# Narrow projections as column strips, and matrix memory's first products ahead of an output gate slot

## The reference, cut to what matters

```python
p = _split(h @ w_in[l])       # a_cq 256, a_ckv 128, a_krope 32, ..., c_qidx 256, c_kidx 32, c_widx 8, ...
k_rope = _rope(p["a_krope"])  # one 32-wide key for all 4 heads
score  = relu(einsum('bqhd,bkd->bqhk', qidx, kidx))         # 8 index heads, one 32-wide index key
index  = einsum('bqh,bqhk->bqk', widx, score) * idx_scale   # 8 index weights per token
```

```python
aq, ak, av, mq, mk, mv, mo, mg = split(h @ w_in)   # mg: 16 gate columns; mo: 512 output gate columns
i_f, f_f, i_b, f_b = mg + gate_b                   # per token
h_m = mlstm(mq, mk, mv, i, log_sigmoid(f))         # forward and backward, summed
h_m = rms_norm(h_m) * sigmoid(mo)
```

## Time and profile before

| | |
|---|---|
| median of 3 runs | 1643.64 us (1638.76 to 1643.98) |
| the profiled execution | 1640.14 us |
| its span | 1638.5 us |
| mean granted TensorE clock | 0.957 |
| TensorE busy | 1507.0 us, 92% |
| VectorE, ScalarE, GpSimd busy | 569.5, 340.9, 93.9 us |
| HBM | 223 GB/s over the span |

### The profile page before, as it was taken

One profiled execution on the slowest core, in us unless ns is written; L12 is line 12 of the kernel. 1 busy time (PEld: TensorE's weight loads), 2 busy tenths in 40 slices (PEclk: granted clock), 3 DMA queues, 4 the chain that ended last, 5 costly groups with the idle time before them and its releaser, 6 DMA issues.

```text
span 1638.5 us, 27188 instructions
## 1 busy us (share of the span) xinstructions
PE 1507.0 (92%) x11479; PEld 1080.2 (66%) x11479; DVE 569.5 (35%) x1400; ACT 340.9 (21%) x788; POOL 93.9 (6%) x144
## 2 busy tenths in 40 slices
PE   6999999999879999999987799999869998999997
PEld 5777777877644576756436799998746675555554
DVE  2514332523443415706414111111056733233233
ACT  1222211222232113217113000000042214010000
POOL 0010000010100000012002000000010000000000
PEclk8899999999989989998998999999979999999999
DMA  8365535475574621065522999999785043999997
GB/s 268 88 209 177 181 98 145 127 233 181 178 215 143 205 77 52 27 215 165 189 82 104 342 388 389 400 396 395 296 291 196 27 154 117 385 385 386 380 388 284
DMA packets 188237, 367.00 MB, mean 224 GB/s; under 512 B 19101, under 2 KB 145913, under 8 KB 172273
## 3 DMA queue, kind: packets, MB, share of 16 engines
q1 hardware_dynamic: 171552, 322.90, 55.5%
q0 software_dynamic: 10544, 32.48, 6.3%
q10 hardware_dynamic: 6048, 10.31, 1.8%
HBM read 345.26 MB, written 20.41 MB: 223 GB/s over the span
## 4 chain that ended last, share of the span: by engine, by line
PE 78%; DMA 8%; DVE 7%; ACT 4%; issue 1%; SPq 1%; POOL 0%; POOLq 0%; DVEq 0%; ACTq 0%
PE ps_proj L652 30%; PE ps_outp L652 9%; PE ps_proj L1270 7%; PE ps_outp L1270 7%; PE ps_score L1270 6%; DMA ring<-in_exp_w 6%; PE ps_outp L1215 3%; PE ps_outp L1371 2%; PE ps_proj L778 2%; PE ps_score L823 1%; PE ps_turn L805 1%; SPq L3142 1%; PE ps_proj L1117 1%; DMA ring<-in_w_in 1%; PE ps_score L1077 1%
## 5 line engine op out<-in xcount | busy, mean ns | idle before, releaser
L652 PE MATMUL ps_proj<-h_t,ring 128*128 128x256 f32 (+1 forms) x1248 | 346.6, 437 | 7.9 <-DMA ring<-in_w_in 3.6
L652 PEld LDWEIGHTS ps_proj<-h_t,ring 128*128 128x128 f32 x1248 | 243.1, 197 | 105.5 <-issue 70.0
L1270 PE MATMUL ps_proj<-ring,arena 128*32 128x384 f32 (+2 forms) x1760 | 118.3, 387 | 8.4 <-DMA ring<-in_exp_w 4.7
L1270 PE MATMUL ps_score<-ring,arena 128*32 128x384 f32 (+2 forms) x1760 | 115.5, 381 | 4.5 <-DMA ring<-in_exp_w 4.5
L1270 PEld LDWEIGHTS ps_proj<-ring,arena 128*32 128x32 f32 (+1 forms) x1760 | 103.9, 115 | 23.0 <-issue 8.5
L1270 PE MATMUL ps_outp<-ring,arena 128*32 128x384 f32 (+2 forms) x1504 | 112.7, 417 | 3.7 <-DVE arena L2661 2.1
L1270 PEld LDWEIGHTS ps_score<-ring,arena 128*32 128x32 f32 (+1 forms) x1760 | 98.5, 113 | 20.9 <-issue 9.8
L652 PE MATMUL ps_proj<-ring,h_t 128*128 128x256 f32 (+1 forms) x512 | 107.8, 366 | 0.4 <-ACT arena L1862 0.4
L652 PEld LDWEIGHTS ps_proj<-ring,h_t 128*128 128x128 f32 x512 | 91.5, 190 | 16.1 <-issue 5.2
L1682 ACT ACTIVATE arena<-ps_proj 128x512 f32<-128x512 f32 (+1 forms) x68 | 38.9, 576 | 302.2 <-PE ps_proj L652 295.9
L1270 PEld LDWEIGHTS ps_outp<-ring,arena 128*32 128x32 f32 (+1 forms) x1504 | 81.7, 114 | 27.4 <-DVE arena L2661 3.8
(11 more groups left out here) (382 smaller groups left out, 1890.2 us busy)
## 6 DMA issues: line engine op xcount, KB each, us to landing
ring<-in_exp_w SPq DMA_DIRECT2D x138, 1024.0 KB, 11.6
ring<-in_ada_w SPq DMA_DIRECT2D x48, 1024.0 KB, 5.8
ring<-in_w_in SPq DMA_DIRECT2D x30, 1024.0 KB, 6.4
arena<-in_exp_w SPq DMA_DIRECT2D x24, 1024.0 KB, 18.6
ring<-in_even_w_in SPq DMA_DIRECT2D x12, 1024.0 KB, 8.8
ring<-in_w_out SPq DMA_DIRECT2D x8, 1024.0 KB, 5.1
row_store<-in_exp_w SPq DMA_DIRECT2D x8, 1024.0 KB, 17.9
x_t<-in_exp_w SPq DMA_DIRECT2D x16, 512.0 KB, 17.4
```

What stands on the lines that cost most here:

```text
L652: last = pe.matmul(out, w, a, start=(i == 0), stop=(i == len(pairs) - 1))
L1270: last = pe.matmul(b[p0:p0 + pn, c0:c0 + wn], x_of(p0, lo, pn), w(w0, wn), start=first and p0 not in strip[:i], stop=done and p0 not in st ...
```

## The change

1. **Strips in the first block (both layers).** `a_ckv` is a chain of its own. Then, for each of the 8 chunks, three narrow matmuls go to three strips of one `proj` bank: the 32 rope key columns to partitions 0 to 31, the 32 index key columns to 32 to 63, the 8 index weight columns to 64 to 71. ScalarE copies the first strip four times, the second four times and the third once (nine copies of 256 columns). Two small matmuls against the identity turn the index weights token-major, and VectorE scales them. The two VectorE copies that repeated the weights, and `rep_ready`, are gone.
2. **Gates in four strips.** The gate slot is loaded as two DMAs, 16 columns twice, side by side with a pitch of 32. Eight matmuls with 32 stationary columns and 512 tokens moving go to four strips in turn, two to a strip. ScalarE copies the bank to `root[:, 0]`. After the first half of `mq`, four matmuls against the constant `quarters` add up the strips and turn them token-major; then comes the second half of `mq`.
3. **Matrix memory.** `products(0)` stands before the second output gate slot. On ScalarE, `products(0)`, `weights(0)` and `weights(1)` stand before the emptying of that slot. `wgt_of[1]` moves from `h_t` to the place of the neighbourhood keys, which are no longer used. The output gates are copied raw, `col` gets its `Exp` from PSUM, and one `Sigmoid` over all 2048 columns follows after the last step, ahead of the switch to `Sqrt`; `gated_head` waits for it (`mo_ready`).

```diff
-        for c0, n in [(256 * c, 256) for c in range(6)] + [(3072, 16), (1536, 256)]:
-            add(((0, KC, n), k_cols(ew, c0, n)))
+        for c in range(6):
+            add(((0, KC, 256), k_cols(ew, 256 * c, 256)))
+        add(*[((c, KC, 16, 32), k_cols(ew, 3072, 16)) for c in (0, 16)])
+        add(((0, KC, 256), k_cols(ew, 1536, 256)))
...
-        wgt_of = [t3(4, T2), h_t[:, 0:4 * T2].rearrange("p (j t) -> p j t", j=4)]
+        wgt_of = [t3(4, T2), arena[:, 2048:4096].rearrange("p (j t) -> p j t", j=4)]
...
 # TensorE, first block
-                chain(b[:, 0:S], [(w[:, k, 0:P], h1[:, k, :]) for k in range(KC)])
-                pe.wait_ge(rep_ready, 2 * l + 1)
-                chain(b[:, S:2 * S], [(kr_w[:, k, :], h1[:, k, :]) for k in range(KC)]).then_inc(filled["proj"], 1)
...
-                chain(b[:, 0:S], [(ki_w[:, k, :], h1[:, k, :]) for k in range(KC)])
-                for t in range(NB):
-                    last = chain(b[:, S + 8 * t:S + 8 * t + 8],
-                                 [(h1[:, k, t * P:(t + 1) * P], w[:, k, 32:40]) for k in range(KC)])
+                for k in range(KC):
+                    for q, w in enumerate((ckv[:, k, P:P + 32], kidx[:, k, 0:32],
+                                           kidx[:, k, 32:40])):
+                        last = pe.matmul(b[32 * q:32 * q + (8 if q == 2 else 32), 0:S], w, h1[:, k, :], start=(k == 0), stop=(k == KC - 1))
...
+                for t in range(NB):
+                    last = pe.matmul(b[:, 8 * t:8 * t + 8], widx_raw[64:72, t * P:(t + 1) * P], ident[64:72, 64:72],
+                                     start=True, stop=True)
...
 # TensorE, gates
-            for t in range(4):
-                last = chain(b[:, 16 * t:16 * t + 16], [(h2[:, k, t * P:(t + 1) * P], w[:, k, :]) for k in range(KC)])
+            for k in range(KC):
+                q = 32 * (k % 4)
+                last = pe.matmul(b[q:q + 32, :], w[:, k, :], h2[:, k, :],
+                                 start=(k < 4), stop=(k >= 4))
...
-            feature_major(h2, T2)
+            for c in range(2):
+                b = claim("proj")
+                chain(b[:, :], [(w[:, k, c * P:(c + 1) * P], h2[:, k, :]) for k in range(KC)]).then_inc(filled["proj"], 1)
+                if c == 0:
+                    got("outp", mark["gate_strips"])
+                    b = claim("outp")
+                    for t in range(4):
+                        last = pe.matmul(b[:, 16 * t:16 * t + 16], root[:, 0, t * P:(t + 1) * P], cst("quarters"),
+                                         start=True, stop=True)
...
 # TensorE, matrix memory
-            feature_major(h2, T2)
-            k_m = use["proj"]
-            got("proj", k_m)
...
+            got("proj", use["proj"] - 1)
             products(0)
+            feature_major(h2, T2)
...
 # ScalarE, first block
+                for r in range(4):
+                    act.activation(ckv_kr[32 * r:32 * r + 32, 1, :], b[0:32, 0:S], ACT.Copy)
+                act.activation(widx_raw[64:72, :], b[64:72, 0:S], ACT.Copy)
+                for r in range(4):
+                    ins = act.activation(kidx_t[32 * r:32 * r + 32, :], b[32:64, 0:S], ACT.Copy)
...
 # ScalarE, matrix memory
             for c in range(2):
-                evac(mo_t[:, c, :], ACT.Sigmoid)
+                evac(mo_t[:, c, :])
...
-            for c in range(2, 4):
-                evac(mo_t[:, c, :], ACT.Sigmoid)
...
             weights(0)
+            weights(1)
+            for c in range(2, 4):
+                evac(mo_t[:, c, :])
...
-                if i + 1 < STEPS:
+                if i and i + 1 < STEPS:
                     weights(i + 1)
...
+            act.activation(mo_t[:, :, :], mo_t[:, :, :], ACT.Sigmoid).then_inc(mo_ready, 1)
             warm_up(ACT.Sqrt)
...
 # VectorE, first block
-                for i, (dst, n, lo) in enumerate(((kr_w, 160, P), (ki_w, 40, 0))):
...
-                    dve.tensor_copy(dst.rearrange("p k (r c) -> p k r c", r=4), src).then_inc(rep_ready, 1)
```

More of the change, by code:

```diff
@@ L459, in k_cols, with slot_view @@
             return w.rearrange("(k p) n -> p k n", p=P)[:, :, c0:c0 + n]
-        def slot_view(buf, k, n, base=0):
-            return ring[:, buf, base:base + k * n].rearrange("p (k n) -> p k n", k=k)
+        def slot_view(buf, k, n, base=0, pitch=None):
+            pitch = pitch or n
+            return ring[:, buf, base:base + k * pitch].rearrange("p (k n) -> p k n", k=k)[:, :, 0:n]
         def add(*parts):
@@ L829, in _ @@
                 feature_major(h1, S, ready=mixer_input())
-                buf = weights()
-                w = slot_view(buf, KC, 160)
+                ckv = slot_view(weights(), KC, 160)
                 b = claim("proj")
-                chain(b[:, 0:S], [(w[:, k, 0:P], h1[:, k, :]) for k in range(KC)])
-                pe.wait_ge(rep_ready, 2 * l + 1)
-                chain(b[:, S:2 * S], [(kr_w[:, k, :], h1[:, k, :]) for k in range(KC)]).then_inc(filled["proj"], 1)
-                done_with("proj")
[L838 to L843, removed]
-                chain(b[:, 0:S], [(ki_w[:, k, :], h1[:, k, :]) for k in range(KC)])
-                for t in range(NB):
-                    last = chain(b[:, S + 8 * t:S + 8 * t + 8],
-                                 [(h1[:, k, t * P:(t + 1) * P], w[:, k, 32:40]) for k in range(KC)])
-                last.then_inc(filled["proj"], 1)
-                done_with("proj")
+                chain(b[:, 0:S], [(ckv[:, k, 0:P], h1[:, k, :]) for k in range(KC)]).then_inc(filled["proj"], 1)
+                slot[0] += 1
+                kidx = slot_view(weights(), KC, 40)
+                b = claim("proj")
[3 more added lines that the diff above has]
+                        last = pe.matmul(b[32 * q:32 * q + (8 if q == 2 else 32), 0:S], w, h1[:, k, :], start=(k == 0), stop=(k == KC - 1))
+                last.then_inc(filled["proj"], 1)
+                slot_end[slot[0] - 1] = (filled["proj"], use["proj"])
+                done_with("proj")
+                k_ckv = use["proj"]
                 feature_major(h1, S)
@@ L1045, in _ @@
             k_nv = use["proj"]
-            w = slot_view(weights(), KC, 16)
+            w = slot_view(weights(), KC, 32)
             b = claim("outp")
-            for t in range(4):
-                last = chain(b[:, 16 * t:16 * t + 16], [(h2[:, k, t * P:(t + 1) * P], w[:, k, :]) for k in range(KC)])
+            for k in range(KC):
+                q = 32 * (k % 4)
+                last = pe.matmul(b[q:q + 32, :], w[:, k, :], h2[:, k, :],
+                                 start=(k < 4), stop=(k >= 4))
             last.then_inc(filled["outp"], 1)
             done_with("outp")
-            feature_major(h2, T2)
+            mark["gate_strips"] = use["outp"]
+            w = slot_view(weights(), KC, 256)
+            for c in range(2):
+                b = claim("proj")
+                chain(b[:, :], [(w[:, k, c * P:(c + 1) * P], h2[:, k, :]) for k in range(KC)]).then_inc(filled["proj"], 1)
+                if c == 0:
+                    got("outp", mark["gate_strips"])
+                    b = claim("outp")
+                    for t in range(4):
+                        last = pe.matmul(b[:, 16 * t:16 * t + 16], root[:, 0, t * P:(t + 1) * P], cst("quarters"),
+                                         start=True, stop=True)
+                    last.then_inc(filled["outp"], 1)
+            done_with("proj")
             pe.wait_ge(head_ready, 8)
@@ L1870, in _ @@
                 evac(nv[:, t:t + 2, 256:512])
+            act.wait_ge(head_ready, 7)
+            act.wait_ge(filled["outp"], mark["gate_strips"])
+            act.activation(root[:, 0, :], bank["outp"][(mark["gate_strips"] - 1) % 2][:, :], ACT.Copy
+                           ).then_inc(drained["outp"], 1)
+            evac(mq_t[:, 0, :], scale=64 ** -0.5)
             act.wait_ge(gate_abs_ready, 1)
@@ L1873, in _ @@
             act.activation(g_soft, g_soft, ACT.Ln, bias=1.0).then_inc(gate_soft_ready, 1)
-            for c in range(2):
-                evac(mq_t[:, c, :], scale=64 ** -0.5)
+            evac(mq_t[:, 1, :], scale=64 ** -0.5)
             for r in (i_row, f_row):
@@ L2301, in _ @@
                 rotate(krot, ckv_kr[:, 1, :], b, krot_ready)
+                b = take("outp")
+                dve.tensor_scalar(widx.rearrange("p a b -> p (a b)"), b[:, 0:16], IDX_SCALE, None, ALU.mult
+                                  ).then_inc(drained["outp"], 1)
+                dve.wait_ge(drained["outp"], use["outp"])
                 dve.wait_ge(krot_ready, l + 1)
@@ L2619, in gated_head @@
                 b = take("turn")
+                if h == 0:
+                    dve.wait_ge(mo_ready, 1)
                 dve.scalar_tensor_tensor(out=ym_t[:, h, :], in0=b[:, :], scalar=col_of("ml_g", h), in1=mo_t[:, h, :],
@@ L3122, in load @@
             def load(buf, part):
-                (base, k, n), src = part
```

(3 more changed lines are left out.)

24 lines of the change are left out of this document (9 added, 15 removed).

## The result

The changed kernel takes 1612.34 us (median of 4 runs, 1611.3 to 1614.02), the kernel before beside it 1641.2 us; the ratio is 0.9834, with a 95% interval of 0.9804 to 0.9864, so 22 to 32 us less. The forecast was 1607.5 us, by a sum of 34.1 us: the measured median lies 4.8 us above it, 0.3 us outside the forecast's own range (1601 to 1612) and inside the whole range (1600 to 1622). The profiled execution took 1612.0 us with a span of 1610.4, 28.1 us less than before.

A forecast was written before the change was run, and what follows sets the result against it. TensorE, busy 92% of the span, was taken as the bound. Gains of 16.0 (strips), 10.9 (gates) and 7.2 us (matrix memory) sum to 34.1, from 1640.14 to 1606.0; median taken as 1607.5 us, own range 1601 to 1612, whole range 1600 to 1622.

The forecast's parts named there:

- The rival without overlap: First block: strips of 32, 32 and 8 columns run one behind another; gain 2.2 instead of 16.0 us, 1621 us; chance 0.11.
- the lower rate: First block's strips: at the skill page's 2.38 times they would take 4.4 us and two layers gain 14.6 us.
- The turn: First block: turning the index weights takes 4 instructions of 0.11 us, 0.45 us a layer.
- The cover of the nine copies: First block: ScalarE's nine copies, 3.4 us a layer, are hidden under the `c_qidx` slot with 3.7 us to spare.
- The bounds given for this part (5.0 and 9.0): Matrix memory gain: 5.0 us if only the first values' start moves, 9.0 if products cost bare 3.36 and nothing waits.
- The Sigmoid's 3.25 us: Matrix memory's end: Sigmoid 1.97 plus table load 1.28 us fit ScalarE's 3.81 us idle time, 0.5 us left.
- 16.0 + 10.9 + 7.2 = 34.1 us: Whole kernel: gains of first block's strips, gates in four strips and matrix memory, added to the total forecast gain.
- the later pairs have no gap to lose: Matrix memory behind `products(1)`: `weights(2)` starts when the first values end, so the 7.2 us gain stays.
- the clock stays low behind the strips: Behind first-block and gate strips: low clock as behind the short matmuls, costing 6.5 us, 1614 us; chance 0.09.
- Absorbed by the experts' loads: Experts: if weight loading sets their end, the program's end wouldn't move, 1641 us; chance 0.05.
- the prediction's sign for it: Distance from even layer's matrix memory end to program end: unchanged if forecast holds, grown if experts' loads absorb the gain.
- Slower through a late `most`: Matrix memory: `most` lands later and TensorE waits; 16 us net at 60 us later, 1657 us; chance 0.03.

The follow-up runs named there:

- again: The changed kernel run a second time with no edit: 1612.6 us, ratio 0.9813 to the kernel before.
- rot_early: The changed kernel with key rotation and index weights' turn right behind the strips, before the slot `c_qidx`, in both layers: 1624.21 us, ratio 0.99.
- defer_only: The changed kernel with the old matrix memory order (second output gate slot, then `products(0)`), keeping raw copies, late Sigmoid and Exp from PSUM: 1615.07 us.
- pad_one: The changed kernel with one useless matmul of 512 columns at the head of the second output gate slot: 1606.4 us, ratio 0.9798.
- gates_late: The changed kernel with the four matmuls that add up the gate strips behind the second half of `mq`: 1615.77 us, ratio 0.9852.
- weave: The changed kernel with two `b_k` matmuls behind each group of index scores, in both layers: 1609.97 us, ratio 0.9809.

## Why the prediction was right, with a gain 6 us too large

**Part 1, strips.** Forecast 3.7 us for three strips of unlike width, measured 3.65. The rival without overlap falls, and so does the lower rate: 24 matmuls of 0.43 us in 3.65 are 2.8 times, where the Trainium skill ("TensorE: Matmul & The Clock Gate", Measured speedup vs the span model) has 2.38 for three column strips, with 512 moving columns; for these matmuls the measurement decides. The turn cost 0.61 instead of 0.45 us. In layer 1 the way to the scores shortened by 7.7 us, for 8.0 forecast. In layer 0 it was 7.1 - 0.7 = 6.4, since `a_cq` and `a_ckv` had more of the low clock in this execution (13.45 us against 12.21; `again` had 12.76). Both together 14.0 for 16.0. The cover of the nine copies was real, by `rot_early`.

**Part 2, gates.** Forecast 10.9 us, measured 27.60 - 16.68 = 10.9. The clock behind the strips stayed at 1.00, against that rival. `gate_ready` came 3.2 us before TensorE was there, for 1.6 to 2.9 forecast.

**Part 3, matrix memory.** Forecast 7.2 us between the second output gate slot and the third values, measured 39.18 - 31.34 = 7.8 (695.75 to 727.09). The low clock in the third values themselves lies behind that mark, and the whole stage fell by 6.7. The bounds given for this part (5.0 and 9.0) don't come out of its terms: with the first values' start alone moving it is 5.4, with bare products 8.4. `defer_only` shows the order to be the cause. The Sigmoid's 3.25 us were 3.19 and lay in ScalarE's idle time, with 0.58 us left for 0.5 forecast.

**What was mis-sized** is the sum, "16.0 + 10.9 + 7.2 = 34.1 us", by a term that it put at nothing. It counted low clock only where the edits remove it and took every untouched stage as unchanged ("Behind `products(1)` ... the later pairs have no gap to lose, so 7.2 stays"). The edited stages gained 14.0 + 10.9 + 7.8, 32.7 us; 28.1 reached the end. Everything else took 4.6 us more on balance: 6.6 more (index scores 1.5 and 0.4, the rest of the matrix memory 1.2, output projection 1.7, router 1.0, experts 0.7) and 2.0 less, 1.4 of it in the modulation ahead of the gates. That piece was luck: without it the forecast gain would have been over 7 us too large and not 6. Wherever the groups were compared one by one (index scores, third values, output projection slot), it is the same instructions at a lower clock. The rival "the clock stays low behind the strips" had the low clock, but in another place. That these pieces aren't fixed is shown by the repeated profiles for the first block, and for the output projection by one profile each of `pad_one`, `gates_late` and `weave`. The rule for when they come stays open.

**The other rivals.** Absorbed by the experts' loads: the prediction's sign for it was that the distance from the matrix memory to the end grows, and it did grow, from 844.7 to 848.2 us. But 2.7 of these 3.5 us lie ahead of the experts, behind the same waits (1.7 of them are the half slot at a low clock), and the experts to the end took 743.6 us after 742.9, with TensorE's waits there for expert weights no longer than before. The sign couldn't tell absorption from low clock. The end of the matrix memory itself came 31.6 us earlier (793.8 to 762.2), for 34 forecast. The DMA share of the chain fell from 8 to 5%. Slower through a late `most`: TensorE never waited for it.

## What to carry to other kernels

Give narrow results strips of one bank, of unlike width too, if the copies that spread them have a slot of dense matmuls over them; and put a matmul group whose results start a long chain on ScalarE and VectorE ahead of an independent slot, not behind it. When stages move in a kernel that TensorE bounds, count a few pieces of low clock of 1 to 2 us each as movable in both directions, put them into the range (the experts' stage alone, edited nowhere, took 740 to 747 us in these profiles; how much of that is clock wasn't taken apart), and profile the same kernel twice before explaining a difference of that size. Where groups of short matmuls wait for ScalarE in between and run at a low clock, weave dense ones between them, but in groups that keep the overlapping ones next to each other.

## What the runs showed of the hardware that was not expected

- With one extra matmul of 0.87 us the stage that holds it and those behind it were 2.9 us shorter, and with two as long as with none (matrix memory, output projection and router: 167.4 us without, 164.5 with one, 167.5 with two).
- The half slot of the output projection took 8.83 us in some kernels and 7.13 in others that are the same from the matrix memory on; in one of these the second output gate slot took 16.83 instead of 14.00 us.
- The unaltered kernel's index scores and the slot behind them took 17.6, 16.5 and 14.8 us in three profiles, with the same waits.
- Two groups of 32-row matmuls on different row strips took 1.14 us next to each other, and one alone 1.13 us.
